# A hybrid state-space and mixture-of-experts layer: triangular masks folded into another matmul, and one of three threshold counts on ScalarE

## The reference, cut to what matters

```
seg = a_cum[:, :, :, None] - a_cum[:, :, None, :]
decay_in = jnp.exp(jnp.where(lower, seg, -jnp.inf))
cb = jnp.einsum('bclgn,bcsgn->bclsg', cc, bc)
y_diag = jnp.einsum('bclgsr,bcsgrp->bclgrp', cb[..., None] * decay_in, X)
```

## Time and profile before

| | |
|---|---|
| median of 3 runs | 2274.65 us |
| the profiled execution: its time | 2273.49 us |
| its span, from first to last instruction | 2270.0 us |
| mean granted TensorE clock | 0.981 |
| TensorE busy | 2164.0 us (95%) |
| VectorE, ScalarE, GpSimd busy | 1347.9, 989.8, 240.2 us |
| `prelude` | 531 to 540 us |
| `mixer` | 540 to 932 us |
| `selection` | 932 to 979 us |

### The profile page before, as it was taken

The page is one execution under the profiler, slowest core; times in us unless marked ns, Lnnn a source line. Parts: engine busy times, 40 slices in busy tenths (PEclk is TensorE's granted clock), DMA queues, the critical chain, the costliest instruction groups (busy, mean ns, idle before and its releaser), DMA issues.

```text
span 2270.0 us, 39605 instructions
## 1 busy us (share of the span) xinstructions
PE 2164.0 (95%) x15677; PEld 2010.6 (89%) x15677; DVE 1347.9 (59%) x2072; ACT 989.8 (44%) x1719; POOL 240.2 (11%) x308
## 2 busy tenths in 40 slices
PE   3999999998999999779999999999999999999996
PEld 1878888896888887679999999999999999999995
DVE  2758554344777776676565656655565556465575
ACT  3743221124555554035344544444444445444653
POOL 1410000013111110110000000000000000000113
PEclk9999999999999999889999999999999999999998
DMA  8633344366334442245666665666665666666795
GB/s 277 228 102 136 134 144 152 100 210 220 107 121 136 153 151 100 75 131 179 182 196 204 174 194 186 208 176 188 194 205 158 201 193 192 183 191 202 244 309 190
DMA packets 320589, 398.69 MB, mean 176 GB/s; under 512 B 11726, under 2 KB 273246, under 8 KB 318702
## 3 DMA queue, kind: packets, MB, share of 16 engines
q1 hardware_dynamic: 290894, 290.36, 40.1%
q0 software_dynamic: 25440, 98.64, 14.1%
q10 hardware_dynamic: 4160, 8.39, 1.1%
HBM read 320.22 MB, written 77.14 MB: 175 GB/s over the span
## 4 chain that ended last, share of the span: by engine, by line
PE 53%; ACT 1%; DVE 1%; issue 1%; DMA 0%; POOL 0%; ACTq 0%; DVEq 0%; POOLq 0%
PE experts_ps_r L2560 50%; PE experts_ps_o L2550 1%; PE experts_ps_x L2540 1%; ACT experts_whi L2635 1%; PE experts_ps_i L2467 0%; ACT experts_junk L2669 0%; DMA experts_xg<-normed,experts_idx 0%; DVE experts_wlo L2798 0%; DVE kept_raw L2906 0%; DVE experts_hid L2970 0%; DVE experts_xg L2906 0%; DVE experts_xg L2915 0%; DVE experts_xlo L2855 0%; PE experts_ps_r L1927 0%; POOL experts_yo L2371 0%
## 5 line engine op out<-in xcount | busy, mean ns | idle before, releaser
L2798 DVE TENSOR_TENSOR experts_wlo<-kept_raw,experts_whi 128x2048 fp32r<-128x2048 f32 x192 | 439.8, 2291 | 389.6 <-ACT experts_whi L2635 389.6
L2560 PE MATMUL experts_ps_r<-experts_xhi,experts_whi 128*128 128x272 f32 x2048 | 603.8, 295 | 7.6 <-DVE experts_xlo L2855 5.1
L2560 PE MATMUL experts_ps_r<-experts_xhi,experts_wlo 128*128 128x272 f32 x2048 | 594.4, 290 | 0.0
L2560 PE MATMUL experts_ps_r<-experts_xlo,experts_whi 128*128 128x272 f32 x2048 | 591.1, 289 | 0.0
L2560 PEld LDWEIGHTS experts_ps_r<-experts_xhi,experts_whi 128*128 128x128 f32 x2048 | 387.3, 189 | 8.2 <-DVE experts_xlo L2855 5.4
L2560 PEld LDWEIGHTS experts_ps_r<-experts_xlo,experts_whi 128*128 128x128 f32 x2048 | 388.0, 189 | 0.0
L2560 PEld LDWEIGHTS experts_ps_r<-experts_xhi,experts_wlo 128*128 128x128 f32 x2048 | 386.9, 189 | 0.0
L2635 ACT ACTIVATE experts_whi<-kept_raw 128x2048 fp32r<-128x2048 f32 x192 | 366.1, 1907 | 0.0
L2560 PE MATMUL experts_ps_r<-experts_hhi,experts_whi 128*128 128x272 f32 x1024 | 301.4, 294 | 2.0 <-DVE experts_hlo L2973 1.9
L2560 PE MATMUL experts_ps_r<-experts_hhi,experts_wlo 128*128 128x272 f32 x1024 | 296.3, 289 | 0.0
L2560 PE MATMUL experts_ps_r<-experts_hlo,experts_whi 128*128 128x272 f32 x1024 | 294.7, 288 | 0.0
(11 more groups left out here) (502 smaller groups left out, 3199.9 us busy)
## 6 DMA issues: line engine op xcount, KB each, us to landing
kept_raw<-in_w_gate SPq DMA_DIRECT2D x64, 1024.0 KB, 5.4
kept_raw<-in_w_up SPq DMA_DIRECT2D x64, 1024.0 KB, 5.4
kept_raw<-in_w_down SPq DMA_DIRECT2D x64, 1024.0 KB, 5.4
shared_whalf<-in_w_ada SPq DMA_DIRECT2D x16, 1024.0 KB, 5.1
ssd_mz<-mixed SPq DMA_DIRECT2D x17, 768.0 KB, 8.3
mixed<-front_acc POOLq DMA_DIRECT2D x12, 1024.0 KB, 4.1
resid<-early_xin POOLq DMA_DIRECT2D x17, 512.0 KB, 5.1
ssd_xs<-resid SPq DMA_DIRECT2D x17, 512.0 KB, 4.0
```

Source lines behind the costliest of these rows:

```text
L2560: mm = pe.matmul(dst, w[:, c % RING, kk, cols], r[:, kk, :], start=(kk == 0 and q == 0), stop=(kk == KD - 1 and q == 2))
L2798: dve.tensor_tensor(wlo[:, c % RING, :, :], raw[:, c % RAW, :, :], whi[:, c % RING, :, :].bitcast(F32), ALU.subtract).then_inc(wlo_done, 1)
```

## The change

1. **The masks.** `negf`, `negb` and their four matmuls per chunk go. Rows 64 to 127 of `acum_t`, until now zeros, hold 2 x 32 coarse bars (0 or -1e30, one for each group of four tokens), and the same rows of `pick` hold `rungs`, which tell which group a token is in. So the four matmuls of a quad bring a mask that is right except within groups of four beside the diagonal. After the exps, GpSimd's `blank` sets what lies on the wrong side of the diagonal to zero, one select of 128x512 f32 per quad, and `mask_sum` waits for `masked` in place of `exp_done`. `prelude` builds bars and rungs: more on GpSimd, one memset on VectorE, and half of `pick` on ScalarE.
2. **The order in the mixer.** `mask_products` comes before `weigh_x` in every chunk. Quads 2 and 3 of chunk 0 have banks of their own (`b5`, `b1`), so they wait for no exp; two folds move into turn(0). The context's states are copied by ScalarE, turned behind the first quads of chunk 1 and copied out by VectorE behind combine(0). Of the four low parts of plain `w_out`, two move from GpSimd to VectorE. The router's weights are scaled a chunk later. The preload of ScalarE's table at the head of the mixer goes.
3. **The selection.** ScalarE counts the third mark, as a sum of signs with an accumulator; TensorE brings it into the same sums by a second small matmul with -0.5 in place of 1, ahead of the first, and the digit is found against `reach`, a bound for each mark. ScalarE's row copies become halves between the counts.

```diff
+BAR, N_BAR, BARS = 4, P // 4, 2 * P // 4
...
+            pool.memset(rungs[:, :, :], 1.0).then_inc(masks_made, 1)
+            pool.wait_ge(masks_made, 1)
+            pool.affine_select(out=rungs[:, :, :], in_=rungs[:, :, :], compare_op=ALU.is_ge, fill=0.0, base=BAR * BARS,
+                               pattern=[[P, 2], [1, P]], channel_multiplier=-BAR).then_inc(masks_made, 1)
+            pool.wait_ge(masks_made, 2)
+            pool.affine_select(out=rungs[:, :, :], in_=rungs[:, :, :], compare_op=ALU.is_ge, fill=0.0, base=BAR - 1 - BAR * BARS,
+                               pattern=[[-P, 2], [-1, P]], channel_multiplier=BAR).then_inc(masks_made, 1)
             pool.tensor_copy(g.identb[:, :], g.ident[:, :]).then_inc(masks_made, 1)
-            pool.memset(g.acum_t[:, :], 0.0).then_inc(zeros_made, 1)
-            pool.wait_ge(masks_made, 3)
-            pool.affine_select(out=g.negf[:, :], in_=g.negf[:, :], compare_op=ALU.is_ge, fill=NEG, base=0,
-                               pattern=[[1, P]], channel_multiplier=-1)
-            pool.affine_select(out=g.negb[:, :], in_=g.negb[:, :], compare_op=ALU.is_ge, fill=NEG, base=0,
-                               pattern=[[-1, P]], channel_multiplier=1)
+            pool.memset(bars[:, :, :], 0.0).then_inc(masks_made, 1)
+            pool.wait_ge(masks_made, RUNGS + 2)
+            pool.affine_select(out=bars[:, 0, :], in_=bars[:, 0, :], compare_op=ALU.is_ge, fill=NEG, base=BAR * BARS,
+                               pattern=[[1, P]], channel_multiplier=-BAR).then_inc(masks_made, 1)
+            pool.affine_select(out=bars[:, 1, :], in_=bars[:, 1, :], compare_op=ALU.is_ge, fill=NEG, base=BAR - 1 - BAR * (BARS + N_BAR),
+                               pattern=[[-1, P]], channel_multiplier=BAR).then_inc(masks_made, 1)
+            pool.wait_ge(masks_made, RUNGS + 4)
+            last = slice(BARS + N_BAR, P)
+            pool.tensor_copy(bars[last, 0, :], bars[last, 1, :]).then_inc(masks_made, 1)
+            pool.wait_ge(masks_made, RUNGS + 5)
+            pool.tensor_copy(g.acum_t[BARS:P, :].rearrange("p (n t) -> p n t", t=P),
+                             bars[BARS:P, 0:1, :].broadcast_to([P - BARS, NT, P])).then_inc(masks_made, 1)
...
+            act.wait_ge(masks_made, RUNGS)
+            for sem, value in g.mixed_stored:
+                act.wait_ge(sem, value)
+            act.activation(g.pick[BARS:P, :, :].rearrange("p (w h) l -> p w h l", w=2),
+                           rungs[BARS:P, :, :].unsqueeze(2).broadcast_to([P - BARS, 2, H, P]), ACT.Copy)
+            act.wait_ge(stack_chain, 7)
...
+            dve.memset(g.acum_t[BARS // 2:BARS, :], 0.0).then_inc(stack_chain, 1)
             for sem, value in g.mixed_stored:
                 dve.wait_ge(sem, value)
-            dve.tensor_copy(g.pick[:, :, :], pick_col[:, :].unsqueeze(2).broadcast_to([P, HH, P]))
+            dve.tensor_copy(g.pick[0:BARS, :, :], pick_col[0:BARS, :].unsqueeze(2).broadcast_to([BARS, HH, P]))
...
-        fold_bank = (b67[:, 0, :], b67[:, 1, :], b34[:, 0, :], b34[:, 1, :], b0[:, :], b67[:, 0, :], b67[:, 1, :], b34[:, 1, :])
+        fold_bank = (b67[:, 0, :], b67[:, 1, :], b0[:, :], b34[:, 0, :], b34[:, 1, :], b67[:, 0, :], b67[:, 1, :], b34[:, 1, :])
+        def quad_bank(i, q):
+            return b34[:, q % 2, :] if i or q < 2 else (b5[:, :], b1[:, :])[q - 2]
...
+            def blank(i):
+                for q in range(4):
+                    rows = ex[:, q, :].rearrange("p (h l) -> p h l", l=P)
+                    way = 1 if q < 2 else -1
+                    pool.wait_ge(S["exp_done"], 4 * i + q + 1)
+                    pool.affine_select(out=rows, in_=rows, compare_op=ALU.is_ge, fill=0.0, base=0,
+                                       pattern=[[0, 4], [way, P]], channel_multiplier=-way).then_inc(S["masked"], 1)
+            blank(0)
             skip(0)
-            for kk in range(4, KD):
+            for kk in range(4, 6):
...
+                    blank(1)
+                    skip(1)
...
+                if 0 < i < NT - 1:
+                    blank(i + 1)
...
-                            pe.wait_ge(S["fold_lo"], (4, 8)[i - 1])
-                    else:
+                            pe.wait_ge(S["low_made"], 4 + q if i == 1 else 9)
+                    elif i:
                         pe.wait_ge(S["exp_done"], 4 * i + q - 1)
-                    neg = (g.negf, g.negb)[q // 2]
-                    pe.matmul(b34[:, q % 2, :], g.identb[:, :], neg[:, :].unsqueeze(1).broadcast_to([P, 4, P]),
-                              start=True, stop=False, skip_group_check=True)
                     for hh in range(4):
-                        ins = pe.matmul(b34[:, q % 2, P * hh:P * hh + P], g.pick[:, 4 * q + hh, :], g.acum_t[:, cols(i)],
-                                        start=False, stop=True, skip_group_check=True)
+                        ins = pe.matmul(quad_bank(i, q)[:, P * hh:P * hh + P], g.pick[:, 4 * q + hh, :], g.acum_t[:, cols(i)],
+                                        start=True, stop=True)
...
+                if i == 0:
+                    fold(0)
+                    fold(1)
+                    pe.wait_ge(S["exp_done"], 4)
...
-                    pe.wait_ge(S["so_copied"], 2)
-                    for d, src in enumerate((y2, o)):
-                        for a in range(4):
-                            ins = pe.transpose(b67[:, d, P * a:P * a + P], src[:, P * a:P * a + P], g.ident[:, :])
-                    ins.then_inc(S["so_turned"], 1)
+            def turn_states():
+                pe.wait_ge(S["so_copied"], 2)
+                for d in range(2):
+                    for a in range(4):
+                        at = 512 * (1 - d) + P * a
+                        ins = pe.transpose(b67[:, d, P * a:P * a + P], o[:, at:at + P], g.ident[:, :])
+                ins.then_inc(S["so_turned"], 1)
...
+                        pe.wait_ge(S["low_made"], 9)
                     pe.wait_ge(S["mlo_done"], i + 1)
                 elif i:
                     pe.wait_ge(S["xb_done"], i)
                 for kk in range(KD):
+                    if i == 0 and half == 0 and kk >= 4:
+                        if kk < 6:
+                            pe.wait_ge(S["wo_lo"], kk - 3)
+                        else:
+                            pe.wait_ge(S["low_made"], kk + 3)
...
-            act.preload_act_table_set("natural_log_exp_and_others")
...
+            act.wait_ge(S["s_done"], 1)
+            act.activation(o[:, 512:1024], b2[:, :], ACT.Copy).then_inc(S["so_copied"], 1)
+            act.wait_ge(S["so_mm"], 1)
+            act.activation(o[:, 0:512], b67[:, 0, :], ACT.Copy).then_inc(S["so_copied"], 1)
...
-                dve.wait_ge(S["exp_done"], 4 * i + 4)
+                dve.wait_ge(S["masked"], 4 * i + 4)
...
-                if i == 0:
-                    dve.wait_ge(S["s_done"], 1)
-                    dve.tensor_copy(y2[:, :], b2[:, :]).then_inc(S["so_copied"], 1)
-                    dve.wait_ge(S["so_mm"], 1)
-                    dve.tensor_copy(o[:, 0:512], b67[:, 0, :]).then_inc(S["so_copied"], 1)
-                    dve.wait_ge(S["so_turned"], 1)
-                    dve.nop().then_inc(S["hf_done"], 1)
...
+            def states_out():
+                dve.wait_ge(S["so_turned"], 1)
+                for d in range(2):
+                    dve.tensor_copy(sto[:, d, :], b67[:, d, :]).then_inc(S["so_out"], 1)
+            def plain_low(kk):
+                dve.wait_ge(S["wo_hi"], kk - 3)
+                dve.tensor_tensor(g.wolo[:, kk, :], g.wraw[:, kk, :], g.wohi[:, kk, :].bitcast(F32), ALU.subtract
+                                  ).then_inc(S["low_made"], 1)
...
             mask_sum(0)
+            mask_products(0)
+            for f in range(3):
+                fold_low(f)
             weigh_x(0)
-            mask_products(0)
-            for f in range(FOLDS):
+            for f in range(3, FOLDS):
...
+                if i == 0:
+                    states_out()
...
+                    if i == 0:
+                        plain_low(6)
                     mask_sum(i + 1)
+                    mask_products(i + 1)
                     weigh_x(i + 1)
-                    mask_products(i + 1)
...
+                    plain_low(7)
...
-                if i == 0:
+                if i == 1:
...
+N_DVE = NC - 1
+HALF_ULP = 1 << 15
...
+                    mark = ((c + 1) << (BITS - STEP * (n + 1))) - (0 if c < N_DVE else HALF_ULP)
+                    pool.memset(bits[:, n, c:c + 1], mark).then_inc(made, 1)
...
+            pool.memset(reach[:, 0:N_DVE], float(CAP_L)).then_inc(made, 1)
+            pool.memset(reach[:, N_DVE:NC], float(CAP_L - LAT // 2)).then_inc(made, 1)
...
+            def count_signs(n):
+                act.wait_ge(marked, n + 1)
+                marks = bits[:, 0, :].bitcast(F32) if n == 0 else (cand[:, :].bitcast(F32) if n < NTOP else cand_f[:, :])
+                with nc.allow_low_precision(reason="integers up to 256"):
```

(35 more changed lines are left out.)

71 lines of the change are left out of this document (36 added, 35 removed).

## The result

The new kernel took 2255.98 us (median of 4 runs, 2254.97 to 2258.33), the old one beside it 2275.57 (2273.41 to 2277.98): ratio 0.9915, 95% interval 0.9898 to 0.9932, 19.6 us less. Forecast were 2253.7 us and 20.9 us less. The profiled execution took 2254.97 us, 2253.2 of it span; the old one's took 2273.49 and 2270.0.

A forecast was written before the change was run, and what follows sets the result against it. TensorE's issue bounds the steady mixer, a VectorE and ScalarE chain the first chunks, VectorE's rounds the selection. 12.8 + 3.0 + 5.4 - 0.3 = 20.9 us off 2273.49 gives 2252.6, plus 1.2 for the median: 2253.7 us, range 2249 to 2264.

The forecast's parts named there:

- TensorE's issue bounds the steady mixer: Steady mixer: matmuls removed from TensorE's queue leave the time, 0.88 us per chunk, 12.8 us in all.
- The select at 0.70: Mixer masks: one GpSimd select of 128x512 takes 0.70 us, bounds 0.60 and 1.18.
- xk ahead of mask_sum, mask_sum 2.1, scan 1.1 to spare: Steady chunk: GpSimd's xk takes SBUF first, mask_sum needs 2.1 us, and 1.1 us are spare before scan.
- The turning point at b = 1.46: Mixer: from select time b = 1.46 us on, TensorE waits before scan, 2 us per us of b.
- The forward selects are out of the way: Mixer: forward selects have project's whole first half, some 6 us, so only the backward ones count.
- slower than before: Mixer rival: selects stall TensorE until the 20.9 us gain is spent, at b = 2.15; 2285 at b = 2.5; chance 0.05.
- The filling, 3.0 us: First chunks: project(0) starts near 574.3 instead of 577.41, 3.0 us kept, bounds 0 and 5.0.
- TensorE is free near 573: Filling: TensorE is free near 573, before low(0) ends near 574.2, so project(0) starts near 574.3.
- Selection 5.4 us: Selection: 15 rounds save 0.40 us each, 6.0, less 0.5 for the digit and 0.1 for memsets: 5.4 us.
- The rival of a starved clock: Selection rival: at 1.2 GHz a round costs 2.5 instead of 1.65; four more such rounds lose 3.4 us, 2257; chance 0.13.
- Prelude -0.3: Prelude: added GpSimd work and VectorE's memset lose 0.3 us, range 0 to 1.7.
- The experts are untouched: Experts behind the selection: they start when the positions are known and are untouched, 0 us.

The follow-up runs named there:

- e1: New kernel with one bf16 matmul of 512 columns put back ahead of each quad from chunk 2 on, selects kept; 2270.7 us, ratio 0.9969 to old.
- e2: New kernel with each of the mixer's selects from chunk 3 on done three times (b = 1.95 us); 2309.4 us, ratio 1.0146 to old.
- e5: New kernel with each of the mixer's selects from chunk 3 on done twice (b = 1.28 us); 2266.5 us, median of nine executions, ratio 0.9977 to old.
- e8: New kernel with 16 transposes of the identity on TensorE ahead of scan(1); 2254.8 us, ratio 0.9914 to old.
- e12: New kernel with the context's index matmuls ahead of the experts' first fillers and 16 transposes ahead of scan(1); 2250.99 us, ratio 0.9897 to old.
- e3: New kernel with the old selection, four counts on VectorE and none on ScalarE; 2263.4 us, ratio 0.9953 to old.
- e11: New kernel with fewer filler transposes between the selection's rounds (4, 6 instead of 7, 11); 2256.4 us, ratio 0.9913 to old.
- e4: New kernel with the context's two index matmuls ahead of the 20 filler transposes at the experts' start; 2253.4 us, ratio 0.99 to old.
- e7: New kernel with weigh_x ahead of mask_products again, the old order; 2258.5 us, ratio 0.9931 to old.
- e10: New kernel unchanged, run again to see which parts repeat; 2254.7 us, ratio 0.991 to old.
- e6: New kernel with the mixer's selects from chunk 3 on done three times and the store of normed behind selects and xk; 2269.7 us, ratio 0.9985 to old.

## Why the prediction was right, point by point

*TensorE's issue bounds the steady mixer.* Shown by e1. The term was 12.8, measured 11.7: the steady 0.87 us came in 13 periods (chunks 4 to 16), and the one into chunk 3 gave 0.37 (20.01 to 19.64), since that one was not yet TensorE's alone.

*The select at 0.70, taken from the row of the same instruction.* 0.637 us in the median of 68 (one took 1.28), near the 0.60 of the lower bound.

*xk ahead of mask_sum, mask_sum 2.1, scan 1.1 to spare.* All as measured (2.06 and 1.2).

*The turning point at b = 1.46.* Wrong in its reason. "The forward selects are out of the way" overlooked that on GpSimd's queue the store of `normed`, held by VectorE, stands ahead of them. The point is near 1.05, and past it each us of b costs four, not two (e2, e5). The rival "slower than before", put at b = 2.15, would have come sooner: 1.95 was 53 us slower than the new kernel and 34.7 slower than the old. The used b = 0.64 lies below both points, so the forecast stood; at the forecast's own upper bound of 1.18, which it called hidden, the loop would by estimate have cost 4 x (1.18 - 1.05) = 0.5 us a chunk.

*The filling, 3.0 us.* The first project matmul was to come 3.1 earlier; 1.1 came (37.17 to 36.09 after the mixer's start). VectorE's part went as forecast: low(0) ended at 573.14, forecast 574.2. What failed was "TensorE is free near 573": after its 3.2 us wait for the product it was granted 1.2 GHz and reached project at 575.93. e8, which takes only that away, brings it to 34.6, right behind low(0), and e12 to 33.5. The forecast took TensorE's clock in the filling as given, and by the stretch from scan(1) to project that is worth 2.7 us. Nor is 1.1 a firm number: in the six profiles with the new kernel's mixer unedited the first project lies between 35.2 and 38.2 after the mixer's start, on both sides of the old kernel's 37.2, of which there is one profile. So that the filling gained anything without e8's edit is not shown.

*Selection 5.4 us.* 6.5 in the profiles, and e3, with the old selection, loses it again. The counts gave 0.40 a round as forecast (2.05 to 1.63 is 0.42, so the digit's second tensor cost nothing), and the rounds at 1.2 GHz went away, which the text had named as worth 0.5 more. The rival of a starved clock, put at four rounds of 2.5, did not happen in either profile of the new kernel; in five other profiles it did for one round, at 2.3 to 2.4 and 0.5 to 0.7 us in all. e11 shows that the price is mostly that of the fillers.

*Prelude -0.3.* As measured, 9.27 for 8.99. Three other profiles with the same prelude (e4, e7, e8) have 10.3 to 10.4, which lies within the stated 0 to 1.7.

*"The experts are untouched."* The step that was missing. Their first fillers ran at 1.2 GHz, which moved a gather by 1.8 us behind the start of a 2.3 us instruction of VectorE. Gains not claimed (tail 2.95, outside the span 1.7, selection 1.1, before the prelude 0.7) covered it in this execution, and that is luck: the tail is 52.0 again in e10, and the 1.7 belong to one execution of the old kernel. That the total came within 2.3 us of the forecast is to that extent chance, though the two largest terms were right for their reasons. How the medians' 19.6 us split beyond the profiled executions is not known. That the old kernel does not have this loss rests on its one profile; why its fillers ran at full clock, and those of every profile of a new kernel at 1.2 GHz for some of their time, stays open. That the selection is not the cause is shown (e3).

## What to carry to other kernels

Work handed to GpSimd starts when its queue lets it, not when its input is there: list what stands ahead on the queue and whom that waits for, and look for a loop before trusting a slack. Fillers that keep TensorE's clock up belong behind the small matmul that a chain waits for. Where a descriptor-generating DMA on GpSimd and a long two-input VectorE instruction are within tenths of a us of each other, keep them apart by order: 0.2 us decided 3.8 us at the next stage's first matmul between e2 and e5, and 3.1 at its end. And take the same kernel's profile twice before giving a few us of one stage to a change: the tail and the filling moved by 3 us with no edit.

## What the runs showed of the hardware

A GpSimd select of 128x512 in f32 takes 0.63 to 0.65 us, and 1.03 to 1.09 beside VectorE instructions of the same size with two SBUF inputs, which then take 1.00 instead of 0.69 (e6, at 739 to 742); xk takes 1.04 with VectorE waiting for it, where the forecast had worked out 0.90. The issue of the experts' first indirect gathers on GpSimd takes 0.94 to 1.09 us, and 2.68 to 3.08 when it begins behind the start of VectorE's low part. ScalarE's sign over 256 columns takes 0.51 and its accumulator's read 0.19. The same code in the mixer's tail takes 49.1 us in three profiles (the new kernel, e3, e8), 50.8 in e12 and 51.9 to 52.3 in the rest: TensorE is at 1.00 and 0.83 in the new kernel's where e7's has a stretch at 0.71, and the new kernel has 49.1 and, in e10, 52.0 with no edit between them.
